# Two output projections as seven products of half sums in place of eight block products

## The reference, cut to what matters

```
h = rms_norm(x); q, k, v, z = h @ w_in          (even: sliding window, block attention, memory;
y = concat(attention heads) * silu(z)            odd: forgetting attention, memory)
return x + y @ w_out                             y: 512 x 1024, w_out: 1024 x 1024
```

## Time and profile before

| quantity | value |
|---|---|
| time, median of 3 runs | 1146.78 us (1146.63 to 1147.28) |
| span of the profiled execution | 1144.8 us |
| PE busy | 1139.4 us, 6154 matmuls |
| DVE, ACT, POOL busy | 669.3, 597.5, 144.5 us |
| granted TensorE clock | 0.999 of full speed |
| first output stage | 811.29 to 858.48 us |
| second output stage | from 1096.11 us; last matmul starts at 1141.28 us |

### The profile page before, as it was taken

The page is one execution under the profiler, slowest core; times in us unless marked ns, Lnnn a source line. Parts: engine busy times, 40 slices in busy tenths (PEclk is TensorE's granted clock), DMA queues, the critical chain, the costliest instruction groups (busy, mean ns, idle before and its releaser), DMA issues.

```text
span 1144.8 us, 15674 instructions
## 1 busy us (share of the span) xinstructions
PE 1139.4 (100%) x6154; PEld 946.6 (83%) x6154; DVE 669.3 (58%) x1174; ACT 597.5 (52%) x1052; POOL 144.5 (13%) x153
## 2 busy tenths in 40 slices
PE   9999999999999999999999999999999999999998
PEld 8888888888888888888889888777888888877887
DVE  5584523488745676524547677577445674776631
ACT  5533431234436766733337577777433687577720
POOL 1000000000000000000000004444223000622531
PEclk9999999999999999999999999999999999999999
DMA  6423323233232221332435233212223323122221
GB/s 193 131 76 109 106 79 115 88 97 110 94 109 56 92 93 38 127 110 74 158 137 129 74 107 78 74 39 75 74 74 112 110 74 114 63 81 83 70 74 74
DMA packets 108081, 107.91 MB, mean 94 GB/s; under 512 B 18076, under 2 KB 93212, under 8 KB 108008
## 3 DMA queue, kind: packets, MB, share of 16 engines
q1 hardware_dynamic: 106504, 101.67, 28.9%
q10 hardware_dynamic: 1504, 5.24, 1.2%
HBM read 104.64 MB, written 2.25 MB: 93 GB/s over the span
## 4 chain that ended last, share of the span: by engine, by line
PE 98%; ACT 1%; DMA 0%; DVE 0%; issue 0%; DVEq 0%; ACTq 0%
PE acc L1772 24%; PE acc L1773 24%; PE acc L1774 24%; PE aux L1772 3%; PE aux L1774 3%; PE aux L1773 3%; PE aux L2211 3%; PE aux L2199 3%; PE acc L2175 3%; PE aux L2004 1%; PE aux L2006 1%; PE aux L2005 1%; PE aux L1864 1%; PE aux L2055 1%; PE aux L2054 1%; PE acc L2190 0%
## 5 line engine op out<-in xcount | busy, mean ns | idle before, releaser
L1772 PE MATMUL acc<-ht_hi,whi 128*128 128x512 f32 x712 | 277.9, 390 | 0.0
L1774 PE MATMUL acc<-ht_hi,wlo 128*128 128x512 f32 x712 | 277.2, 389 | 0.0
L1773 PE MATMUL acc<-ht_lo,whi 128*128 128x512 f32 x712 | 277.1, 389 | 0.0
L1204 DVE TENSOR_TENSOR wlo<-raw,whi 128x2048 fp32r<-128x2048 f32 x68 | 155.6, 2289 | 108.7 <-ACT whi L776 103.2
L700 POOL TENSOR_SCALAR whi<-raw 128x512 fp32r<-128x512 f32 x68 | 49.0, 721 | 940.8 <-DMA raw<-e_w_in_dram 705.1
L776 ACT ACTIVATE whi<-raw 128x2048 fp32r<-128x2048 f32 x68 | 129.9, 1910 | 53.0 <-DMA raw<-w_in_dram 22.6
L1774 PEld LDWEIGHTS acc<-ht_hi,wlo 128*128 128x128 f32 x712 | 133.7, 188 | 28.0
L1772 PEld LDWEIGHTS acc<-ht_hi,whi 128*128 128x128 f32 x712 | 133.7, 188 | 27.6 <-DVE wlo L1204 0.2
L1773 PEld LDWEIGHTS acc<-ht_lo,whi 128*128 128x128 f32 x712 | 133.7, 188 | 27.1
L701 POOL TENSOR_TENSOR wlo<-raw,whi 128x512 fp32r<-128x512 f32 x68 | 92.0, 1354 | 5.7
L1772 PE MATMUL acc<-whi,ht_hi 128*128 128x512 f32 (+1 forms) x224 | 83.9, 375 | 0.0
(11 more groups left out here) (290 smaller groups left out, 2040.5 us busy)
## 6 DMA issues: line engine op xcount, KB each, us to landing
raw<-w_in_dram SPq DMA_DIRECT2D x72, 512.0 KB, 4.6
raw<-o_w_in_dram SPq DMA_DIRECT2D x28, 512.0 KB, 4.7
raw<-e_w_in_dram SPq DMA_DIRECT2D x14, 512.0 KB, 5.0
raw<-w_proj_pool_dram SPq DMA_DIRECT2D x8, 512.0 KB, 4.0
raw<-w_proj_mlstm_dram SPq DMA_DIRECT2D x8, 512.0 KB, 4.0
raw<-w_out_dram SPq DMA_DIRECT2D x8, 512.0 KB, 4.3
raw<-o_w_out_dram SPq DMA_DIRECT2D x8, 512.0 KB, 4.6
raw<-e_w_in_dram SPq DMA_DIRECT2D x14, 256.0 KB, 3.9
```

What stands on the lines that cost most here:

```text
L1204: v.tensor_tensor(wlo[:, slot, :], raw[:, slot, :], whi[:, slot, :].bitcast(F32), ALU.subtract).then_inc(w_split, 1)
L1772: mm(out_, w_hi_, x_hi, start=first, stop=False)
L1773: mm(out_, w_hi_, x_lo, start=False, stop=False)
L1774: return mm(out_, w_lo_, x_hi, start=False, stop=last)
```

## The change

With y cut into four blocks (A11: tokens 0 to 255, channel tiles 0 to 3; A12: the same tokens, tiles 4 to 7; A21 and A22: tokens 256 to 511) and w_out into B11, B12, B21, B22 of 512 x 512, the projection becomes seven products, in this order on PE: A11 B11; S3 T3; A12 B21; S2 T2; S1 T1; S4 B22; A22 times T4, where S1 = A21 + A22, S2 = S1 - A11, S3 = A11 - A21, S4 = A12 - S2, T1 = B12 - B11, T3 = B22 - B12, T2 = B22 - T1 and T4 = B21 - T2. Each is 4 channel tiles x 2 groups of 128 tokens (e) x 3 = 24 matmuls of the same shape as before. Banks keep their sums, and are added to the residual rows between products, as soon as a sum belongs to a block of the result.

- POOL makes S3 (`third_sum`), T3, T1 and T4 (`out_weights`), and splits three units a layer (A11_B11, S3_T3, A12_B21).
- DVE makes the other sums (`first_sums`, `out_by_seven`) and T2 (`second_weight_mix`); ACT and DVE split the four later weights and three half sums (`staged_weight_head`, `half_sum_head`, and the rests). `first_sums`, two residuals and `second_weight_mix` stand in step 17 of the loop, ahead of `gated_out(7)`.
- SP loads seven quarters of w_out a layer instead of four: three into slots, and B12, B11, B22 and B21 into w_keep and w_again, which lie over tiles that are free by then. The y tiles are kept over the query tiles instead of in zT.
- The memory rows are fetched by ACT in step 17 into another place. Units 71 and 72 (o_mem) wait for S1_T1 and S4_B22 to be done. The stores are five.

```diff
--- before.py
+++ after.py
+        half_sums = [(at(f"half_sum{n}_hi", [P, 4, UC], HT + 8 * n * K, F32R), at(f"half_sum{n}_lo", [P, 4, UC], HT + (8 * n + 4) * K, F32R))
+                     for n in range(3)]
+        sum_raw = at("sum_raw", [P, 4, UC], R0 + 12 * K)
+        sum_less = [at("sum_less_e", [P, 4, UC], R1 + 16 * K), at("sum_less_o", [P, 4, UC], R1 + 20 * K)]
+        w_keep = [at("w_keep_e", [P, SLOT], R3), at("w_keep_o", [P, SLOT], R1 + 12 * K)]
+        w_again = [at("w_again_e", [P, SLOT], R1 + 24 * K), at("w_again_o", [P, SLOT], R1 + 28 * K)]
+        memrow_again = at("memrow_again", [P, MT, D], HT + 24 * K)
+        w_mixed = at("w_mixed", [P, SLOT], R0 + 4 * K)
...
+                                  ("e_z", 4, 4), ("e_out", 7, 2), ("o_mem", 2, 2), ("o_f", 1, 1),
+                                  ("o_qk", 7, 7), ("o_v", 3, 3), ("o_z", 4, 4), ("o_out", 7, 2)):
...
+        SEVEN = (0, 1)
+        OUT = {L: plan["eo"[L] + "_out"] for L in SEVEN}
+        OUT_UNITS = {OUT[L][0] + u: (SEVEN.index(L), u) for L in SEVEN for u in range(7)}
+        X_READS, TERMS, LATE = 6, 10, 4
+        KEPT = AGAIN = ((48, 80), (112, 144))
+        A11_B11, S3_T3, A12_B21, S2_T2, S1_T1, S4_B22, A22_T4 = range(7)
...
+            def stage_sevenfold(L, view):
+                n, before, at_ = OUT[L][0], L * NP, SEVEN.index(L)
+
+                def into_slot(u, col, kh):
+                    slot_free(n + u)
+                    slot = (n + u) % SLOTS
+                    quarter(L, view, raw4[:, slot, :, :], col, kh, w_loaded[slot])
+                keep, again = (w[L][:, :].rearrange("p (k c) -> p k c", k=4) for w in (w_keep, w_again))
+                into_slot(A11_B11, 0, 0)
+                sp.wait_ge(logit_ready, before + 16)
+                quarter(L, view, keep, WIDE, 0, keep_in)
+                into_slot(S3_T3, WIDE, 1)
+                sp.wait_ge(o_ready, before + 24)
+                quarter(L, view, again, 0, 0, again_in)
+                into_slot(A12_B21, 0, 1)
+                sp.wait_ge(t1_ready, at_ + 1)
+                quarter(L, view, again, WIDE, 1, again_in)
+                sp.wait_ge(term_w_split, LATE * at_ + 2)
+                quarter(L, view, keep, 0, 1, keep_in)
+            stage_sevenfold(0, wview(A["e_w_out_2"][0]))
 
...
+            def third_sum(L):
+                for k in range(4):
+                    y, late = y_tile(L, k), slice(UC, S)
+                    pool.wait_ge(t_ready, 32 + 8 * L + k + 1)
+                    step(nc.gpsimd.tensor_tensor(op_raw[:, k, late], y[:, 0:UC], y[:, late], ALU.subtract))
+                    step(nc.gpsimd.tensor_scalar(op_hi[:, k, late], op_raw[:, k, late], 1.0, 1.0, ALU.mult, ALU.mult))
+                    nc.gpsimd.tensor_tensor(op_lo[:, k, late], op_raw[:, k, late], op_hi[:, k, late].bitcast(F32),
+                                            ALU.subtract).then_inc(s3_ready, 1)
...
+            def out_weights(L):
+                n, at_ = OUT[L][0], SEVEN.index(L)
+                split(n + A11_B11)
+                slot = (n + S3_T3) % SLOTS
+                pool.wait_ge(w_loaded[slot], loaded(n + S3_T3))
+                pool.wait_ge(keep_in, KEPT[L][0])
+                for piece in quarters:
+                    step(nc.gpsimd.tensor_tensor(raw[:, slot, piece], raw[:, slot, piece], w_keep[L][:, piece], ALU.subtract))
+                split(n + S3_T3)
+                pool.wait_ge(again_in, AGAIN[L][0])
+                for piece in quarters:
+                    ins = nc.gpsimd.tensor_tensor(w_keep[L][:, piece], w_keep[L][:, piece], w_again[L][:, piece], ALU.subtract)
+                ins.then_inc(t1_ready, 1)
+                split(n + A12_B21)
+                pool.wait_ge(keep_in, KEPT[L][1])
+                pool.wait_ge(t2_ready, at_ + 1)
+                for piece in quarters:
+                    ins = nc.gpsimd.tensor_tensor(w_keep[L][:, piece], w_keep[L][:, piece], w_mixed[:, piece], ALU.subtract)
+                ins.then_inc(t4_ready, 1)
...
+                def staged_weight_head(u):
+                    n, at_ = OUT[L][0], SEVEN.index(L)
+                    slot = (n + u) % SLOTS
+                    wait_unit_done(act, n + u - SLOTS)
+                    source = {S2_T2: w_mixed, S1_T1: w_keep[L], S4_B22: w_again[L], A22_T4: w_keep[L]}[u]
+                    if u == S2_T2:
+                        act.wait_ge(t2_ready, at_ + 1)
+                    if u == A22_T4:
+                        act.wait_ge(t4_ready, at_ + 1)
+                    nc.scalar.activation(whi[:, slot, :], source[:], ACT.Copy).then_inc(term_w_hi, 1)
+
+                def half_sum_head(m):
+                    act.wait_ge(sum_ready, 2 * SEVEN.index(L) + 1 + m // 2)
+                    nc.scalar.activation(half_sums[m][0][:], (sum_less[L], sum_raw, sum_less[L])[m][:], ACT.Copy).then_inc(sum_hi, 1)
...
-                        act.dma_start(memrow[:], memv).then_inc(mem_in, 16)
+                    if L == 0 and i == NQ + 1:
+                        act.dma_start(memrow_again[:], memv).then_inc(mem_in, 16)
...
+                        j, cols = out_due(i), y_cols(L, out_due(i))
+                        if L in SEVEN and j == KT - 1:
+                            staged_weight_head(S2_T2)
+                        head(y_tile(L, j)[:, cols], op_hi[:, j, cols])
...
+                half_sum_head(0)
+                staged_weight_head(S1_T1)
+                half_sum_head(1)
                 if L == 0:
-                    squares(memrow, memn, MT, 20, lambda t: act.wait_ge(mem_in, 32))
+                    squares(memrow_again, memn, MT, 20, lambda t: act.wait_ge(mem_in, 32))
+                half_sum_head(2)
+                staged_weight_head(S4_B22)
+                if L == 0:
                     heads_of_transposes("o_mem", memT[1][0], MEM, tiles=range(4))
+                staged_weight_head(A22_T4)
...
+                def first_sums(ks):
+                    for k in ks:
+                        dve.wait_ge(t_ready, 32 + 8 * L + k + 5)
+                        ins = v.tensor_tensor(sum_raw[:, k, :], y_tile(L, k)[:, UC:S], y_tile(L, k + 4)[:, UC:S], ALU.add)
+                    step(ins)
+                    for k in ks:
+                        ins = v.tensor_tensor(sum_less[L][:, k, :], sum_raw[:, k, :], y_tile(L, k)[:, 0:UC], ALU.subtract)
+                    return ins
...
+                def second_weight_mix():
+                    at_ = SEVEN.index(L)
+                    dve.wait_ge(t1_ready, at_ + 1)
+                    dve.wait_ge(again_in, AGAIN[L][1])
+                    dve.wait_ge(prT_ready, done + NP)
+                    v.tensor_tensor(w_mixed[:], w_again[L][:], w_keep[L][:], ALU.subtract).then_inc(t2_ready, 1)
...
+                    if i == NQ + 1 and L in SEVEN:
+                        first_sums(range(3))
                     if 2 <= i:
                         turned(A - 3)
+                    if i == NQ + 1 and L in SEVEN:
+                        for e in range(2):
+                            x_into_rows(A11_B11, e, e, 0)
+                        second_weight_mix()
                     if 1 <= i <= NQ:
...
+                        if L in SEVEN and j == KT - 1:
+                            first_sums((3,)).then_inc(sum_ready, 1)
+                            staged_weight_rest(S2_T2)
+                        rest(y_tile(L, j)[:, cols], op_hi[:, j, cols], op_lo[:, j, cols])
...
+                def out_by_seven():
+                    at_, a = SEVEN.index(L), OUT[L][1]
+                    half_sum_rest(0)
+                    staged_weight_rest(S1_T1)
+                    half_sum_rest(1)
+                    z_into_rows(0)
+                    x_into_rows(S2_T2, 0, 2, 0)
+                    dve.wait_ge(sum_ready, 2 * at_ + 1)
+                    for k in range(4):
+                        ins = v.tensor_tensor(sum_less[L][:, k, :], y_tile(L, k + 4)[:, 0:UC], sum_less[L][:, k, :], ALU.subtract)
+                    ins.then_inc(sum_ready, 1)
+                    z_into_rows(1)
+                    x_into_rows(S2_T2, 1, 3, 0)
+                    if L == 0:
+                        y_into_rows(0)
+                        y_into_rows(1)
+                        normalise(memrow_again, memn, MT, 20)
+                    half_sum_rest(2)
+                    staged_weight_rest(S4_B22)
+                    dve.wait_ge(z_read, 2 * at_ + 2)
+                    x_into_rows(S1_T1, 0, 2, 1)
+                    if L:
+                        y_into_rows(0)
+                        y_into_rows(1)
+                    x_into_rows(S1_T1, 1, 3, 1)
...
+                def term(L, u, e, ks=range(4)):
+                    n, a, _ = OUT[L]
+                    bank = {A12_B21: aux[:, e, :], S3_T3: z_pair_bank(L, e), A22_T4: z_pair_bank(L, e)}.get(u, x_bank(L, e))
+                    slot, opens = (n + u) % SLOTS, u in (A11_B11, S3_T3, A12_B21)
+                    for k in ks:
+                        if u in (S2_T2, S1_T1, S4_B22):
```

(35 more changed lines are left out.)

236 lines of the change are left out of this document (158 added, 78 removed).

## The result

| kernel | median of its runs | lowest to highest | ratio to the kernel before |
|---|---|---|---|
| before | 1146.68 us | 1146.57 to 1147.28 | 1 |
| changed | 1149.63 us | 1147.8 to 1153.1 | 1.0027 [1.0017, 1.0037] |

The changed kernel is 3 us slower; the forecast was 1.3 us faster, and rival 2 (the clock falls in the waits, 1149.4) came true. The profiled execution's span grew from 1144.8 to 1148.8 us. The runs of the changed kernel also lie 5 us apart, those of the kernel before 0.7.

A forecast was written before the change was run, and what follows sets the result against it. The prediction took the matmul engine PE as the bound: 10.9 us of matmuls removed, 9.6 returning as waits, E +1.0 and O -2.3, together -1.3 us, so 1145.4 us. The range for 8 in 10 was 1139.5 to 1150.

The forecast's parts named there:

- rival 2: PE's clock falls in the first output stage's (E's) waits, slowing the matmuls behind them: +2.6 us, 1149.4 us; chance 0.20.
- What goes: Both output stages: 24 matmuls fewer per layer, 5.44 us each, 10.9 together; without waits E 41.8 us, O (second stage) 40.0.
- Before the stages, on POOL: Attention loops: POOL's added third sum, subtractions and weight mixes cost nothing, and the loop period stays 13.48 us.
- Block A12_B21: Output stages: late weight loads and DVE's mix stopping POOL's split make PE wait 2.6 us in E, 1.5 in O.
- The chain on DVE: Output stages from the mix on: DVE's queue makes PE wait 3.7 us for S4_B22 in E, 0.9 and 0.7 in O.
- Sum: Both output stages: E 48.2 us against 47.2, O 43.1 against 45.4, together -1.3 us, giving 1145.4 us.
- Rivals 1: Output stages: POOL and DVE collisions are small and new waits short; -8.1 without them, valued at -4.7, 1142.1 us; chance 0.30.
- 3: Output stages: the gain is full, 10.9 us, 1135.9 us; chance 3 in 100, counted within the small-collisions rival.
- 4: Attention loops get longer as DVE's copies wait behind POOL: 16 steps of 0.3 us, 1150.3 us; chance 0.10.
- The collision that I left to the skill: E: DVE's memory-row rescaling may exclude POOL, each waiting up to 1.1 us, E up to 2 us later; not in the total.

The follow-up runs named there:

- experiment 5: Changed kernel with the memory rows' DMA issued by ACT about twelve microseconds later, after T2's head: 1146.14 us, ratio 0.9996.
- experiment 4: Changed kernel with A12_B21's four weight heads made by ACT instead of POOL, in both layers: 1146.82 us, ratio 0.9999.
- experiment 1: Changed kernel with idle matmuls (11 and 12) keeping PE busy in the two waits of the first output stage: 1148.41 us, ratio 1.0015.
- experiment 10: Kernel with seven products in the second layer alone and ACT's heads, plus one PE wait mid-E for two idle ACT copies: 1148.12 us against 1143.42.
- experiment 3: Changed kernel with DVE's T2 subtraction cut to 64 of 2048 columns (output wrong, timing only): 1145.78 us, ratio 0.9990.
- experiment 11: Changed kernel with ACT making A12_B21's heads and scaling memory rows instead of DVE, memory DMA later, DVE's order in E altered: 1140.27 us, ratio 0.9944.
- experiment 6: Changed kernel with S4_B22's rests ahead of DVE's y and memory row work in E, PE's memory transposes moved behind S4_B22: 1158.62 us, ratio 1.0105.

## Why the prediction was wrong

Point by point, by its own steps:

- *What goes.* Right: 48 matmuls are gone, and the stages' floors hold in every row of the table.
- *Before the stages, on POOL.* Right: from E's end to O's start the kernel takes what it took, 237.6 us.
- *Block A12_B21.* Right, in mechanism and nearly in size: landed at 816.8 (forecast 816.3), POOL held up by DVE's mix, split done at 826.8 (826.3), waits of 3.06 us in E and 1.7 us in O (2.6 and 1.5). The landing is right partly by luck: 3.7 us of transfer left at 811.3, at half speed as I wrote, end at 818.7, not at 816.3. What I had as one value is a range: in five profiles with three transfers at once the landing lies between 816.8 and 818.3. That these transfers are behind most of the spread of the times is shown only so far as moving one of them cuts it from 5.3 to 1.6 us (experiment 5); with ACT's heads it is 1.8 us though the three transfers stay (experiment 4).
- *The chain on DVE.* Right in that PE waits for S4_B22, 3.3 us in E and 1.3 in O (forecast 3.7 and 0.9), and a third time in O, 0.47 (0.7). In E the two waits together are 6.36 us, the forecast's 6.3, but this is luck: I had DVE without a gap, residual ready at 847.3 and PE asking at 843.6; DVE stood idle for 2.33 us waiting for PE, PE went on at 849.4 and asked at 846.1, both over 2 us later than forecast.
- *Sum.* **This is the step that failed.** "E: 41.8 + 2.6 + 3.7 + 0.1 = 48.2" lets every matmul behind a wait run at 0.2267 us. The waits alone give 48.1, but the stage took 53.0: the sum lacks a term for the clock, +4.9 us in the profiled execution. Added to the forecast of the spans, with O 0.7 us above its figure (0.3 in its waits, 0.4 in none of them) and E's start 0.3 us sooner, it makes -1.3 + 4.9 + 0.7 - 0.3 = +4.0, the difference of the profiled spans. (1146.78 - 1.3 is 1145.5, not 1145.4.) Keeping PE busy takes the term away (experiment 1), a wait with nothing else about it brings it (experiment 10).
- *Rival 2* had the mechanism, its place, the number of slow matmuls (24 forecast, 19 found) and nearly the time (1149.4 for 1149.63), at a chance of 0.20. The nearness of the time is in part luck: its clock term was 3.9 us, with 1.5 us taken off the second wait, and the profiled run lost 4.9 with no such relief, since the late PE made DVE late as well; the median run is 1.0 us below that one. It was undervalued on one row: "E's two are near the 2.2 us, not far above". The earlier trace rows show a clock that had already fallen 2.2 us after the last matmul; a forecast wait of 2.6 and one of 3.7 us were both beyond it, so the row spoke for the rival. The Trainium skill, "TensorE: Matmul & The Clock Gate", section "HAM oscillation — how this bites in real kernels", says that PE starts cold again after each such wait, with the lost time in proportion to the number of waits. The trace agrees that each wait pays: 0.43 us a matmul, 7 of them behind the first and 12 behind the second. It differs in the start: behind the first wait five matmuls ran at up to 0.33 us before the pitch became 0.43.
- *Rivals 1, 3 and 4* are out: the collisions are there (experiments 3 and 4), and no loop grew.
- *The collision that I left to the skill.* The Trainium skill, "SBUF — State Buffer", section "Who interferes with whom", lets DVE's tensor_scalar exclude POOL. Experiment 4 shows the meeting, on DVE's side: the rescaling takes 1.59 us for 0.75 beside POOL's subtraction. In the changed kernel it starts 0.1 us after T4's end (843.67) and meets nothing; that the sum held nothing for it came out by that little, for in experiments 1, 3, 4 and 5 they meet. (I had priced one POOL operation at 1.1 us; it takes 1.30.)

Why half of a change that removes 10.9 us had to be won back by experiment 11: the matmuls removed were also the time in which DVE and POOL did the new work. E had 47 us with DVE busy for 18; with 5.4 us less and 25 us more on DVE, its queue and not PE sets the second half. Experiment 11 brought the loads sooner, gave ACT the heads of A12_B21 and took two jobs, 1.8 us, off DVE.

Left open: what decides whether a wait of 2 to 3 us costs the clock in a given run (the same kernel does both), and where the 5 us between the runs of the changed kernel come from, run by run, since only one of them was profiled.

## What to carry to other kernels

When work is taken from the bounding engine and given to idle ones, add up the waits and then give each of 2 us and more a price for the clock behind it: here, where it fell, 5 to 12 matmuls at nearly twice their time, 1.5 to 2.5 us. Cut the longest queue rather than the visible wait: of what was saved at E's first wait, a part came back at the second (1.6 of 2.2 us in experiment 4, 0.7 of 1.8 in experiment 5), and moving one engine's step without moving its followers in the other queues cost 9 us (experiment 6). Ask also which engine the filling engine waits for: DVE's own wait for PE carried the first wait into the second. A transfer issued a step later can be worth more than moving an engine's work (3.5 us in experiment 5, 2.8 in experiment 4).
